# Expert weights of a mixture-of-experts layer staged in pairs of pieces, with 16 KB rows per partition

## What is computed

```python
def expert_block(args):
    xi, e = args                      # 128 tokens at most, expert number
    hc = xi @ w1[e] + b1[e]           # 1024 x 2048 weights
    g, u = hc[:, :D_EXPERT], hc[:, D_EXPERT:]
    g = jnp.minimum(g, SWIGLU_LIMIT)
    u = jnp.clip(u, -SWIGLU_LIMIT, SWIGLU_LIMIT)
    hm = (u + 1.0) * (g * jax.nn.sigmoid(SWIGLU_ALPHA * g))
    return hm @ w2[e] + b2[e]         # 1024 x 1024 weights
```

## Time and profile before

| | us |
|---|---|
| median of three runs | 1893.84 |
| profiled execution | 1894.01 |
| its span | 1892.2 |
| profiled execution less its span | 1.8 |

### The profile page before, as it was taken

The page is one execution under the profiler, slowest core; times in us unless marked ns, Lnnn a source line. Parts: engine busy times, 40 slices in busy tenths (PEclk is TensorE's granted clock), DMA queues, the critical chain, the costliest instruction groups (busy, mean ns, idle before and its releaser), DMA issues.

```text
span 1892.2 us, 30544 instructions
## 1 busy us (share of the span) xinstructions
PE 1800.8 (95%) x11046; PEld 1142.9 (60%) x11047; DVE 1019.4 (54%) x1509; ACT 522.9 (28%) x847; POOL 851.9 (45%) x481
## 2 busy tenths in 40 slices
PE   8999999998999999998999999998989999999987
PEld 7999896677899998888733333333333333333332
DVE  6776642345687575758465444444444554444444
ACT  5333443534544345345311011011010111010011
POOL 0000000000000025657277777777777777777774
PEclk9999999999999999999999999999999999999999
DMA  9777442112476643334899999999999999999995
GB/s 347 259 261 266 178 165 103 67 67 90 167 267 237 216 161 134 134 110 158 349 402 419 417 417 418 417 419 416 419 417 401 418 417 419 416 419 417 419 417 216
DMA packets 98894, 560.96 MB, mean 296 GB/s; under 512 B 9008, under 2 KB 11184, under 8 KB 50480
## 3 DMA queue, kind: packets, MB, share of 16 engines
q1 hardware_dynamic: 98688, 560.02, 75.3%
q10 hardware_dynamic: 144, 0.07, 0.0%
HBM read 559.00 MB, written 1.05 MB: 296 GB/s over the span
## 4 chain that ended last, share of the span: by engine, by line
PE 72%; DMA 12%; DVE 8%; ACT 3%; POOL 2%; issue 1%; SPq 0%; DVEq 0%; POOLq 0%; ACTq 0%
PE bank L1219 17%; DMA stage<-w_exp_in 12%; PE bank L676 11%; PE bank L678 11%; PE bank L677 11%; PE bank L1307 9%; POOL ring L1747 2%; DVE cst L1772 2%; PE bank L1230 1%; PE bank L932 1%; DVE cst L2315 1%; PE bank L657 1%; DVE arena L1772 1%; DVE cst L1776 1%; PE bank L1287 1%
## 5 line engine op out<-in xcount | busy, mean ns | idle before, releaser
L1747 POOL COPY ring<-stage 128x2048 f32<-128x2048 f32 x372 | 717.1, 1934 | 245.2 <-DMA stage<-w_exp_in 132.1
L1728 POOL TENSOR_TENSOR w_lo<-ring,w_hi 128x512 fp32r<-128x512 f32 x104 | 134.6, 1328 | 773.3 <-ACT w_hi L1365 773.3
L1219 PE MATMUL bank<-ring,arena 128*64 128x512 f32 x2112 | 471.2, 595 | 8.9 <-POOL ring L1747 8.8
L676 PE MATMUL bank<-x_hi,w_hi 128*128 128x256 f32 (+1 forms) x1336 | 386.2, 289 | 9.1 <-DVE x_lo L1828 4.6
L678 PE MATMUL bank<-x_hi,w_lo 128*128 128x256 f32 (+1 forms) x1336 | 380.4, 285 | 0.0
L677 PE MATMUL bank<-x_lo,w_hi 128*128 128x256 f32 (+1 forms) x1336 | 380.1, 284 | 0.0
L1219 PEld LDWEIGHTS bank<-ring,arena 128*64 128x64 f32 x2112 | 145.0, 136 | 298.3 <-issue 252.6
L676 PEld LDWEIGHTS bank<-x_hi,w_hi 128*128 128x128 f32 x1336 | 253.6, 190 | 24.9 <-issue 15.8
L1792 DVE TENSOR_TENSOR w_lo<-ring,w_hi 128x2048 fp32r<-128x2048 f32 x92 | 210.7, 2290 | 102.9 <-ACT w_hi L1365 100.7
L678 PEld LDWEIGHTS bank<-x_hi,w_lo 128*128 128x128 f32 x1336 | 253.9, 190 | 0.0
L677 PEld LDWEIGHTS bank<-x_lo,w_hi 128*128 128x128 f32 x1336 | 252.9, 189 | 0.1
(11 more groups left out here) (340 smaller groups left out, 2003.5 us busy)
## 6 DMA issues: line engine op xcount, KB each, us to landing
stage<-w_exp_in SPq DMA_DIRECT2D x248, 1024.0 KB, 12.6
stage<-w_exp_out SPq DMA_DIRECT2D x124, 1024.0 KB, 12.8
ring<-stream SPq DMA_DIRECT2D x120, 1024.0 KB, 4.9
arena<-ada SPq DMA_DIRECT2D x48, 512.0 KB, 4.0
ring<-w_exp_in SPq DMA_DIRECT2D x8, 1024.0 KB, 8.1
ring<-w_exp_out SPq DMA_DIRECT2D x4, 1024.0 KB, 14.3
cst<-const_in SPq DMA_DIRECT2D x1, 1584.0 KB, 19.7
arena<-b_exp SPq DMA_DIRECT2D x3, 384.0 KB, 8.3
```

Source lines behind the costliest of these rows:

```text
L676: begin = mm(out_, wh, xh, start=start, stop=False)
L1219: last = mm(bank[2 + gu][pr, :], xT[:, k % 4, k // 4, :], ring[:, k, c0:c0 + 512], start=False, stop=(k == KD - 1), tile_position=pos)
L1728: nc.gpsimd.tensor_tensor(w_lo[:, BUF[p], c:c + REST_COLS], ring[:, p % RING, c:c + REST_COLS], w_hi[:, BUF[p], c:c + REST_COLS].bitcast(f32),
L1747: nc.gpsimd.tensor_copy(ring[:, j, :], stage[:, PLACE[j % STAGED], :]).then_inc(in_place, 1)
```

## The change

The weights lie in HBM in pairs of pieces, so that two neighbouring pieces (0 and 1, 2 and 3, ...) form one row of 16 KB in each partition, for `w_exp_in` and for `w_exp_out` alike. `stage` keeps its size, but is used as three places of two pieces. One DMA moves a pair (2 MB). SP issues it when both pieces that used the place have been copied. POOL still copies piece by piece, with the same copies; it waits for a landing only before the first piece of a pair. The first expert's pieces still go singly to `ring`, now as 8 KB out of the 16 KB rows. Of the first staged loads, a pair goes out after piece 2, the other two pairs after all of the first expert.

```diff
-PLACE = (3, 4, 5, 2, 1, 0)
+PAIR_PLACE = (2, 1, 0)
...
+            def stage_pair(e, pair):
+
+                q = 2 * PAIR_PLACE[pair % 3]
+                sp.dma_start(stage[:, q:q + 2, :].rearrange("p a b -> p (a b)"), expert_pair(e, pair))\
+                    .then_inc(slot_in[2 * pair], 16)
...
-                if j == 1:
+                sp.dma_start(ring[:, j, :], expert_pair(0, j // 2)[:, j % 2 * PIECE:j % 2 * PIECE + PIECE])\
+                    .then_inc(slot_in[j], 16)
+                if j == 2:
                     sp.wait_ge(proj, AT[proj]["o2"] + KD)
+                    sp.wait_ge(x_split, AT[x_split]["w2"] + KD)
                     sp.wait_ge(slot_in[0], loaded[0] + 16)
-                    stage_piece(1, 0)
+                    stage_pair(1, 0)
...
-                for j in range(SLOTS):
-                    sp.wait_ge(in_place, e * SLOTS + (j - STAGED + 1))
-                    stage_piece(expert, j)
+                for pair in range(6):
+                    sp.wait_ge(in_place, e * SLOTS + (2 * pair - 4))
+                    stage_pair(expert, pair)
...
                 for j in range(SLOTS):
-                    pool.wait_ge(slot_in[j], e * 16 + (loaded[j] + 16))
+                    if j % 2 == 0:
+                        pool.wait_ge(slot_in[j], e * 16 + (loaded[j] + 16))
                     pool.wait_ge(freed, before * SLOTS + (DENSE + RING + 1 - SLOTS + j))
                     pool.sem_inc(may_move, 1)
-                    nc.gpsimd.tensor_copy(ring[:, j, :], stage[:, PLACE[j % STAGED], :]).then_inc(in_place, 1)
+                    nc.gpsimd.tensor_copy(ring[:, j, :], stage[:, 2 * PAIR_PLACE[j // 2 % 3] + j % 2, :]).then_inc(in_place, 1)
...
-        "w_exp_in": np.ascontiguousarray(x["w_exp_in_2"][0]).reshape(E * 8, P, 2 * D),
-        "w_exp_out": np.ascontiguousarray(x["w_exp_out_2"][0]).reshape(E * 8, P, D),
+        "w_exp_in": np.ascontiguousarray(
+            x["w_exp_in_2"][0].reshape(E, 4, 2, P, 2 * D).transpose(0, 1, 3, 2, 4)).reshape(E * 4, P, 4 * D),
+        "w_exp_out": np.ascontiguousarray(
+            x["w_exp_out_2"][0].reshape(E, 2, 4, P, D).transpose(0, 1, 3, 2, 4)).reshape(E * 2, P, 4 * D),
```

More of the change, by code:

```diff
@@ L588, in _, with expert_pair @@
                         sp.dma_start(b_raw[i * E:i * E + E, :], b_exp).then_inc(bias_in, 16)
[L590 to L595, removed]
-            loaded = [16 * ROUNDS if s < RING else 0 for s in range(SLOTS)]
[L599 to L604, removed]
+            def expert_pair(e, pair):
+                if pair < 4:
+                    return w_exp_in[bass.ds(e * 4 + pair, 1), :, :].rearrange("o p n -> p (o n)")
+                return w_exp_out[bass.ds(e * 2 + (pair - 4), 1), :, :].rearrange("o p n -> p (o n)")
+            def stage_pair(e, pair):
+                q = 2 * PAIR_PLACE[pair % 3]
+                sp.dma_start(stage[:, q:q + 2, :].rearrange("p a b -> p (a b)"), expert_pair(e, pair))\
+                    .then_inc(slot_in[2 * pair], 16)
+            loaded = [16 * ROUNDS if s < RING else 0 for s in range(SLOTS)]
             for j in (0, 1, 2, 3, 8, 11, 4, 5, 6, 9, 7, 10):
@@ L612, in _ @@
                     sp.wait_ge(proj, AT[proj]["w2"] + KD)
-                dst, src = expert_piece(0, j)
-                sp.dma_start(dst, src).then_inc(slot_in[j], 16)
-                if j == 1:
+                sp.dma_start(ring[:, j, :], expert_pair(0, j // 2)[:, j % 2 * PIECE:j % 2 * PIECE + PIECE])\
+                    .then_inc(slot_in[j], 16)
+                if j == 2:
                     sp.wait_ge(proj, AT[proj]["o2"] + KD)
+                    sp.wait_ge(x_split, AT[x_split]["w2"] + KD)
                     sp.wait_ge(slot_in[0], loaded[0] + 16)
-                    stage_piece(1, 0)
[L619 to L633, removed]
+                    stage_pair(1, 0)
+            sp.wait_ge(slot_in[2], loaded[2] + 16)
+            stage_pair(1, 1)
+            sp.wait_ge(nat, 1)
+            sp.wait_ge(slot_in[4], loaded[4] + 16)
+            stage_pair(1, 2)
+            for pair in range(3, 6):
+                sp.wait_ge(in_place, SLOTS + 2 * (pair - 3) + 2)
+                sp.wait_ge(slot_in[2 * pair], loaded[2 * pair] + 16)
+                stage_pair(1, pair)
             sp.wait_ge(order_ready, 1)
```

## The result

| | before | changed |
|---|---|---|
| median, us | 1894.62 (4 runs) | 1922.74 (1920.79 to 1930.86, 4 runs) |
| ratio to before | | 1.0152, 95% interval 1.0131 to 1.0172 |
| profiled execution, its span | 1894.01, 1892.2 | 1920.79, 1919.0 |
| granted clock over the span | 0.99 | 0.98 |

The changed kernel is slower, as forecast, by 28 us instead of 19. The stretches of the changed kernel (columns as in Rows 2) show DMA faster, as the layout promised: 428 GB/s against 418 in the earlier trace rows. And around the expert with two blocks (1408 to 1465 us) the DMA engines now stand idle for 40% of the time.

A forecast was written before the change was run, and what follows sets the result against it. Before, PE paced most blocks and DMA the last of each half; changed, DVE's waits for POOL's copies would slow every locked block. Blocks summing to 957.3 us put 19.3 us on 1894.0: 1913 us, range 1881 to 1930.

The forecast's parts named there:

- Rate: DMA's weight transfers: a row costs 9.1 ns besides its bytes, so 16 KB rows give 2.449 us a piece.
- Coarser places: SP issues a pair only after its second piece is copied: 4.3 us a half, 8.6 in all, if DMA bounds ends.
- Copies in twos: POOL's two copies in a row hold both of DVE's two-SBUF-tile operations: blocks take 29.39 us, 27.6 before.
- the other case: DVE's first operation comes during a pair's second copy and ends at about 4.3 us, its second operation at 5.0.
- The lock to six pairs: Through DVE's waits on POOL's copies, a block takes exactly six pairs, 29.39 us, and this repeats.
- The lead: Kernel before: PE's lead of weights shrinks 2.5 us a block; each half's last five or so blocks go at DMA's pace.
- The sum: 33 expert blocks: 27 at 29.39, 4 at 27.11, 2 at 27.64 us, less 0.4, ending at 1894.8 us.
- Rival A: DVE slips between the two copies or PE's phase drifts; blocks stay near 27.6, DMA bounds: 1881.6 us, chance 0.20.
- half locked: The block after block 0 and the one after the double expert take 27.64 us, against 27.11 unlocked and 29.39 locked.
- the fall of the clock: PE's clock falls in every block, some 1.1 us each; taken in by locking, else 30 us more, 1943 us, chance 0.04.

## Why the prediction was right, and where it was short

**Rate.** 2.449 us a piece was forecast, from a cost of 9.1 ns a row. Copies 100 to 160 of the changed kernel come 2.449 us apart on the mean. The DMA records of the traces show the cost of a row by itself: one of 4 KB took 160 ns and one of 8 KB 311 ns in the median (kernel before), one of 16 KB 613 ns (changed), and each is 9 ns less than twice the one before it. The runs with other row lengths gave 422 GB/s for 8 KB throughout and 418 for pairs with old rows. Right, and it is the rows, not the size of the DMA. The estimate from the Trainium skill (page DMA: Bandwidth & Descriptors, section Why small descriptors are slow (HBM only)), 4.94 us a pair, would have been 424 GB/s; 428 was measured.

**Coarser places.** 8.6 us forecast, 9.5 measured (11 in the traces), and not seen in the changed kernel, whose chain has no DMA. Right in size; its two terms, 2.45 us at a restart and 1.87 at an end, were not measured apart.

**Copies in twos.** The mechanism is shown from four sides: made alone in the kernel before (+27 us), taken away in the changed one (-41 us), both together (within a few us), and shortened (-34 us). The order (second copy before L2309) is in the rows. The end of L2309 was forecast at 4.90 us after the pair's first copy and is at 4.73 in the 18 blocks where it is held; in the 11 where L1766 comes during the second copy it is at 5.0, which the prediction gave as the other case. The rule that the prediction took from the Trainium skill, page SBUF — State Buffer, section Who interferes with whom, holds too in its other half: with one operand in PSUM and one in SBUF the DVE operations took 0.70 us beside POOL's copies.

**The lock to six pairs.** Right for the changed kernel: by the ends of L2309 each block takes 29.1 to 29.7 us once the lock stands (29.41 on the mean by the starts), and it is exact where the clock stays up. But the text called it steadier than it is: with pairs of 5.0 us it slips, by the rows above, to a mean of 29.4 to 29.7.

**The lead.** The prediction has the kernel before at the pace of DMA for the last five or so blocks of each half. In its trace five blocks of the first half are 30.1 us apart, but only the last two of the second. The sum of the forecast doesn't use it.

**Rival A** was priced at 1881.6 us. It did not happen, but the kernel with `u` in PSUM is that rival made real, and took 1881.9. That the two agree to 0.3 us is luck, since the medians of the groups move by 2 us.

**Where it was short.** The sum put the end of the last L1300 at 1894.8 us; it is at 1902.2, 7.4 us later. By the starts of the blocks: 0.9 us before the first block, far inside the spread of the dense part; the second block, held by both copies with a fall of the clock on top, 31.0 us where the sum had it half locked at 27.64 (3.4 us); the third 31.0 where it had 29.39 (1.6 us); the thirteen blocks up to the double expert 0.2; the second half's blocks about 1.4 together. Two terms of the sum were too small. The block behind block 0 was not half locked but held by both copies at once. And the fall of the clock, put at nothing, cost about 1.6 us in each of the first two held blocks. The prediction had the locking take it in, and from the fourth block on it did; in these two POOL itself waited for PE's late L1300, so the copies came late as well, and twelve of them took 31.1 us (981.53 to 1012.59) where they later take 29.4:

```profile
989.96 1.89 POOL L1741 COPY ring<-stage 128x2048 f32<-128x2048 f32 x1 [1.64 <-PE bank L1300]
992.40 3.73 POOL L1741 COPY ring<-stage 128x2048 f32<-128x2048 f32 x2 [0.55 <-PE bank L1300]
```

Four small matmuls a block took back 5.1 us in the first seven blocks (200.3 against 205.4 us), 1.7 more up to the double expert, and 0.2 in the second half. The other 2 us are between the profiled execution (1920.8) and the median (1922.7).

## What to carry to other kernels

When a change makes work come in bursts on one engine, look for operations of another that share something with it and fit today into its pauses; a larger transfer can change that pattern on an engine that the diff hardly touches. Keep the operands of a short critical VectorE operation out of the way of GpSimd's long copies (one operand in PSUM was enough here), or cut the long copies. And before paying for coarser handing over, take the part of the gain that has no such cost: here a relaid `w_exp_out` alone was worth 7 us (2 to 12 by its interval).

## What the runs showed that I had not expected

- Two loops of different length, joined only by such a hold, fall into step to within 0.04 us a block (29.35 to 29.39 us). A single unlucky phase, 0.02 us behind a copy's start, costs 3.3 us: two operations of 0.69 us take 2.42 and 2.26.
- The step breaks when the burst's period grows by 0.1 us, and a slower DMA then gives PE hardly slower blocks: 2.2 us more over the whole expert part with pairs of 5.0 us than with pairs of 4.9.
- After a stand of PE of 2.3 to 2.6 us for DVE the granted clock fell in 13 of 18 blocks, and pieces 8 to 11 took up to 8.4 us instead of 6.9. It doesn't follow from the length alone: in the kernel before with copies in twos PE stood 3.28 us in the block at 1052.84, and its pieces 8 to 11 took 6.87 us. Whether the fall costs time depends on who sets the pace behind it.
